# A Mamba-2 convolution tile: four products on ScalarE, three additions on GpSimd

## The reference, cut to what matters

```python
def causal_dwconv(xpad, w, bias):
    K = w.shape[0]
    T = xpad.shape[1] - K + 1
    y = bias
    for j in range(K):
        y = y + xpad[:, j:j + T] * w[j]
    return y

def ssd_mixer(z, xbc, dt_raw, conv_buf, h0, conv_w, conv_b, dt_bias, A_log, D_skip, norm_w):
    ...
    xpad = jnp.concatenate([conv_buf.astype(xbc.dtype), xbc], axis=1)
    xbc_c = jax.nn.silu(causal_dwconv(xpad, conv_w, conv_b))
    ...
    xs, Bm, Cm = jnp.split(xbc_c, [C_INNER, C_INNER + C_GROUPS * C_STATE], axis=-1)
    ...
    y, h_new = ssd_scan(xs, dt, A, Bm, Cm, h0.astype(F32))
```

## Time and profile before

| | |
|---|---|
| median of three runs | 3177.0 us |
| the profiled execution, its own time | 3178.87 us |
| its span | 3177.1 us |
| mean granted TensorE clock | 0.971 of full |
| `local_stage`, first `convolve_x` to last matmul | 1083 to 1372 us |
| PE, DVE, ACT, POOL busy over the span | 94%, 51%, 27%, 24% |

### The profile page before, as it was taken

One profiled execution on the slowest core, in us unless ns is written; L12 is line 12 of the kernel. 1 busy time (PEld: TensorE's weight loads), 2 busy tenths in 40 slices (PEclk: granted clock), 3 DMA queues, 4 the chain that ended last, 5 costly groups with the idle time before them and its releaser, 6 DMA issues. The chain is left out here.

```text
span 3177.1 us, 45320 instructions
## 1 busy us (share of the span) xinstructions
PE 2986.0 (94%) x16451; PEld 2559.2 (81%) x16451; DVE 1618.7 (51%) x3026; ACT 867.5 (27%) x1660; POOL 749.8 (24%) x512
## 2 busy tenths in 40 slices
PE   8999999789899799978979999999998999999998
PEld 5888889666666599866769999999996788888886
DVE  5113211266678488856645555545556444444445
ACT  4223222223332255533342211112213111111112
POOL 4002100134444145522201222111221121122210
PEclk9999999889999899989989999999999999999999
DMA  4455335367674244338652111121113311111101
GB/s 147 165 210 178 111 128 176 91 187 210 196 211 140 86 120 116 88 93 266 199 205 102 40 40 40 40 79 40 40 53 137 115 53 40 40 40 59 60 13 54
DMA packets 237378, 350.26 MB, mean 110 GB/s; under 512 B 75334, under 2 KB 172135, under 8 KB 231256
## 3 DMA queue, kind: packets, MB, share of 16 engines
q1 hardware_dynamic: 236289, 325.80, 33.1%
q0 software_dynamic: 944, 22.61, 1.9%
HBM read 283.53 MB, written 93.97 MB: 119 GB/s over the span
## 5 line engine op out<-in xcount | busy, mean ns | idle before, releaser
L2558 POOL TENSOR_TENSOR cm_dn_lo<-cm_dn_raw,cm_dn_hi 128x1024 fp32r<-128x1024 f32 x44 | 107.8, 2470 | 972.1 <-ACT cm_dn_hi L2607 972.1
L3288 PE MATMUL pj_acc<-pj_w_hi,pj_h_hi 128*128 128x480 f32 (+3 forms) x896 | 335.5, 374 | 0.9 <-DVE pj_h_lo L3163 0.9
L3289 PE MATMUL pj_acc<-pj_w_lo,pj_h_hi 128*128 128x480 f32 (+3 forms) x896 | 333.9, 373 | 0.0
L3290 PE MATMUL pj_acc<-pj_w_hi,pj_h_lo 128*128 128x480 f32 (+3 forms) x896 | 333.7, 372 | 0.0
L2851 PE MATMUL cm_u_ps<-cm_h_hi,cm_up_hi 128*128 128x344 f32 (+1 forms) x880 | 309.5, 352 | 12.6 <-DVE cm_a_lo L2724 12.6
L2851 PE MATMUL cm_g_ps<-cm_h_hi,cm_up_hi 128*128 128x344 f32 (+1 forms) x880 | 310.3, 353 | 11.3 <-DVE cm_h_lo L2663 10.9
L2853 PE MATMUL cm_u_ps<-cm_h_hi,cm_up_lo 128*128 128x344 f32 (+1 forms) x880 | 308.7, 351 | 0.0
L2853 PE MATMUL cm_g_ps<-cm_h_hi,cm_up_lo 128*128 128x344 f32 (+1 forms) x880 | 308.7, 351 | 0.0
L2852 PE MATMUL cm_u_ps<-cm_h_lo,cm_up_hi 128*128 128x344 f32 (+1 forms) x880 | 307.9, 350 | 0.0
L2852 PE MATMUL cm_g_ps<-cm_h_lo,cm_up_hi 128*128 128x344 f32 (+1 forms) x880 | 307.9, 350 | 0.0
L3169 DVE TENSOR_TENSOR pj_w_lo<-pj_w_raw,pj_w_hi 128x480 fp32r<-128x480 f32 (+3 forms) x112 | 75.7, 697 | 377.8 <-ACT pj_w_hi L3125 377.7
(11 more groups left out here) (447 smaller groups left out, 6484.8 us busy)
## 6 DMA issues: line engine op xcount, KB each, us to landing
fp_kv<-in_fox_kv SPq DMA_DIRECT2D x256, 256.0 KB, 3.0
area<-in_w_up SPq DMA_DIRECT2D x44, 1024.0 KB, 7.1
cm_dn_raw<-in_w_down SPq DMA_DIRECT2D x44, 512.0 KB
out_s_win<-in_cache POOLq DMA_DIRECT2D x8, 2047.0 KB, 9.3
proj_a<-pj_row SPq DMA_DIRECT2D x48, 240.0 KB
sp_raw<-proj_b SPq DMA_DIRECT2D x16, 640.0 KB, 4.0
pj_w_raw<-in_w_a SPq DMA_DIRECT2D x10, 960.0 KB, 7.0
dp_raw<-proj_a SPq DMA_DIRECT2D x48, 192.0 KB, 3.8
```

What stands on the lines that cost most here:

```text
L2558: pool.tensor_tensor(dn_lo[:, s], dn_raw[:, s], dn_hi[:, s].bitcast(F32), ALU.subtract).then_inc(dn_ready, 1)
L3288: pe.matmul(out, h_hi[:, k, place(t)], w_hi[:, j % 2, k, 0:wide], start=(k == 0), stop=False)
L3289: pe.matmul(out, h_hi[:, k, place(t)], w_lo[:, j % 2, k, 0:wide], start=False, stop=False)
L3290: last = pe.matmul(out, h_lo[:, k, place(t)], w_hi[:, j % 2, k, 0:wide], start=False, stop=(k == KT - 1))
```

## The change

ScalarE gets a function `multiply_taps`, called in phase 1 behind `sp_z_tanh`. It makes the four products of the third x tile, each into its own part of `sp_x_part`, which grows from one to four tiles; the first product takes the bias with it (Identity with scale and bias, both per-partition), the others are Copy with a per-partition scale. GpSimd's `convolve_x` waits for all four (a new semaphore `taps_done`) and makes three additions. The waits for `xT`, the halo and the earlier readers move to ScalarE with the products; for chunk 0 ScalarE waits for `diag_ready` as well, which comes after the taps were halved. `mask` and everything else stays where it was in its queue.

```diff
-        x_part = sb("sp_x_part", [P, P])
+        x_part = sb("sp_x_part", [P, C_CONV, P])
...
+        taps_done = sem("sp_taps_done")
...
             def convolve_x(c):
-                pool.wait_ge(in_ready, 2 * c + 1)
-                pool.wait_ge(halo_ready, c + 1)
-                if c >= 1:
-                    pool.wait_ge(s_ready, 2 * c - 1)
                 k = XT - 1
-
-                def tap(j):
-                    return taps[:, k, j:j + 1].to_broadcast([P, P])
-
-                gps.link(pool, pool.tensor_tensor(x_conv[:, k], xT[:, c % 2, k, 0:P], tap(0), ALU.mult))
-                gps.link(pool, pool.tensor_tensor(x_conv[:, k], x_conv[:, k], tap(C_CONV), ALU.add))
-                for j in range(1, C_CONV):
-                    gps.link(pool, pool.tensor_tensor(x_part[:], xT[:, c % 2, k, j:j + P], tap(j), ALU.mult))
-                    last = pool.tensor_tensor(x_conv[:, k], x_conv[:, k], x_part[:], ALU.add)
-                    if j < C_CONV - 1:
-                        gps.link(pool, last)
-                last.then_inc(x_conv_ready, 1)
+                pool.wait_ge(taps_done, c + 1)
+                gps.link(pool, pool.tensor_tensor(x_conv[:, k], x_part[:, 0], x_part[:, 1], ALU.add))
+                gps.link(pool, pool.tensor_tensor(x_conv[:, k], x_conv[:, k], x_part[:, 2], ALU.add))
+                pool.tensor_tensor(x_conv[:, k], x_conv[:, k], x_part[:, 3], ALU.add).then_inc(x_conv_ready, 1)
...
+            def multiply_taps(c):
+                k = XT - 1
+                act.wait_ge(halo_ready, c + 1)
+                act.wait_ge(in_ready, 2 * c + 1)
+                if c >= 1:
+                    act.wait_ge(s_ready, 2 * c - 1)
+                else:
+                    act.wait_ge(diag_ready, 1)
+                act.activation(x_part[:, 0], xT[:, c % 2, k, 0:P], ACT.Identity, scale=taps[:, k, 0:1],
+                               bias=taps[:, k, C_CONV:C_CONV + 1])
+                for j in range(1, C_CONV):
+                    last = act.activation(x_part[:, j], xT[:, c % 2, k, j:j + P], ACT.Copy, scale=taps[:, k, j:j + 1])
+                last.then_inc(taps_done, 1)
...
                     act.activation(z_tanh[:], raw[:, now % 2, CZ:CX], ACT.Tanh, scale=0.5).then_inc(z_tanh_ready, 1)
+                    multiply_taps(now)
```

## The result

The changed kernel took 3181.48 us (median of 20 runs, 3174.61 to 3193.5), the kernel before in the same comparison 3177.85: a ratio of 1.0018, with a 95% interval of 1.0009 to 1.0026, or 2.9 to 8.3 us more. 3183.0 was forecast.

What follows compares the result with a forecast made beforehand. In the changed stage TensorE (98% busy) and VectorE (87%) were taken as near their limit. Chunk delays at L1332 sum to +6.2, rounded to +6.0 us, taking the median from 3177.0 to 3183.0; range 3172 to 3190.

Steps and rivals of the forecast that it cites:

- The gauge and the slack: TensorE's wait at turn_x for VectorE's sp_y (L1332): 2.9 us growing to some 9; handover 0.15, slack 0.40 or none.
- the first kind: Chunks 1 to 5 and 9, where VectorE's L1332 comes early for turn_x: 0.40 us of slack each, 2.3 us lost together.
- ScalarE's four products: On ScalarE ahead of copy_out: four 128x128 instructions take 1.36 us, at no cost because ScalarE then idles 2.59 us.
- The added wait: GpSimd's first addition waits for taps_done: starts at 1181.07 against 1180.94 in chunk 5, 1319.87 against 1319.53 in chunk 13.
- The mask and who goes first: GpSimd's mask starts about 2.6 us sooner and goes before VectorE's last L1262 or sp_z: +1.2 us chunk 5, +1.3 chunk 13.
- The relief behind it: VectorE instructions after sp_z, no longer beside the mask, run faster: -0.41 us chunk 5, about -0.65 or -0.85 in later ones.
- The sum: Delay at L1332 over the stage's chunks: 2.3, 0.8, 2.0, 1.35, -0.2 and 0, total +6.2 us, rounded to +6.0.
- Chunk 0: 0: At the stage's start the taps wait for diag, but VectorE and turn_x have over 1.5 us of slack: 0 us.
- (a): Rival, faster: VectorE passes before the mask, TensorE's waits before L1426 vanish, -4.6 us to 3172.4; chance 0.15.
- (b): Rival, no change: the mask wins in some chunks and loses in others, cancelling within 2 us, 3177; chance 0.14.
- (c): Rival, much slower: ScalarE's taps_done comes late, each 0.4 us delaying additions and mask in all 16 chunks, 3189; chance 0.07.
- (d): Rival: ScalarE's Identity wants another table, two loads of 1.28 us a chunk, 3177 + 41 = 3218; chance 0.02.

Runs made afterwards that it cites:

- spare_taps: Kernel before plus ScalarE's four products, written to a tile nothing reads; GpSimd unchanged. Ratio 0.9993, median 3175.9 us.
- changed_again: The changed kernel, unaltered, timed once more beside other runs on one chip. Ratio 1.0005, median 3181.6 us.
- diag_first: Kernel before, with GpSimd's convolve_x of chunk 0 waiting for diag_ready. Ratio 0.9992, median 3176.4 us.
- mask_after_z: Changed kernel, with the mask of chunk c+1 also waiting until VectorE's sp_z of chunk c is done. Ratio 0.9977, median 3170.5 us.
- mask_early_late_start: Changed kernel with the mask moved to phase 0 and the mask of chunk 1 waiting for diag_ready. Ratio 0.9966, median 3167.9 us.
- mask_early: Changed kernel with GpSimd's mask moved from phase 2 to phase 0, behind sp_xdd. Ratio 0.9971, median 3170.9 us.
- adds_alone: Kernel before with GpSimd's eight instructions replaced by three additions, no ScalarE products, computing other numbers. Medians 3178.4 and, repeated, 3177.7 us.
- more_before_mask: Changed kernel plus one unread GpSimd product of 128x384 between the additions and the mask. Ratio 1.003, median 3187.2 us.

## Why the prediction was right

**The gauge and the slack.** Right. The 0.15 handover is there in all chunks of the changed kernel, and the first kind lost its 0.40 of slack before it lost time: the wait before `turn_x` in chunks 1 to 5 and 9 is 0.39 or 0.40 each, 2.4 in sum for the 2.3 forecast.

**ScalarE's four products.** Right: 0.48 and three of 0.39, 1.37 us where 1.36 was forecast. The row of the exponential had given that number. By the formula of the Trainium skill ("ScalarE: Activation LUTs", What ACT_TABLE_LOAD costs) it was 1.36 as well, and this trace agrees with its 0.479 us for the first and 0.386 for each of the others. They cost nothing: the chunks and the stage of spare_taps are as long as those of the kernel before.

**The added wait.** Right: the first addition starts 1.85 us behind the start of `sp_z_tanh` in chunk 5 (1172.73 against 1170.88) and in chunk 13; 1.85 was forecast for both.

**The mask and who goes first.** Right, and this was the guess with the most weight. In chunks 1 to 11 the last tap, in 12 to 14 `sp_z` waited out the mask, in every one of them. `sp_z` ended 1.20 us later in chunk 5 and 1.30 later in chunk 13, counted from `sp_z_tanh`; 1.2 and 1.3 were forecast.

**The relief behind it.** Right. From the end of `sp_z` to that of L1336 it is 4.71 us in chunk 5 instead of 5.10 (-0.39, forecast -0.41), 4.08 in chunk 13 instead of 4.93 (-0.85, as forecast).

**The sum.** By kinds, from the waits before `turn_x`: +2.4 (2.3), chunk 8 +0.8 (0.8), chunks 6, 7, 10 and 11 together +2.0 (2.0), 12 to 14 +1.3 (1.35), chunk 15 -0.2 (-0.2). The distance over all chunks grew by 6.5 for 6.2.

**What was missed** are two terms at the ends, -1.8 and +1.9 us. That they cancel, so that the whole stage too came out 6.6 us longer, is luck. Chunk 0 and the start were put at nothing; the faster build of the diagonal matrices gave 1.8 us back. The step of the prediction that failed is "Chunk 0: 0": I looked for slack behind the products and not at what their going away relieves. And the tail, from the last `sp_xd` to L1518, took 12.6 us instead of 10.7. The granted clock is 0.72 on the mean in 4 us of it, that is a part of the stretch at the lower level (1.2 GHz); before it was 1.00 there. Ahead of the fall TensorE had been idle for 0.69 and 0.89 us, with matmuls between; the kernel before has the same two idle times at this place and kept its level. The clock (last figure but two) in these 4 us and in the whole tail, of the changed kernel and of the kernel before:

```profile
1360.00:1364.00 4.00, 2.85 (x16) 2.71 (x16) 1.17 (x8) 2.13 (x9) 1.76 (x2) 0.72 0.29 83
1357.83:1370.38 12.55, 8.95 (x55) 8.47 (x55) 6.80 (x27) 5.45 (x23) 3.57 (x4) 0.81 0.12 33
```

```profile
1363.00:1367.00 4.00, 2.70 (x24) 2.56 (x24) 2.01 (x14) 2.13 (x9) 2.52 (x3) 1.00 0.34 99
1361.32:1371.98 10.66, 6.90 (x55) 6.42 (x55) 6.72 (x27) 5.45 (x23) 3.56 (x4) 1.00 0.15 40
```

The same 55 matmuls take 8.95 us instead of 6.90, while ScalarE's work is the same and VectorE's nearly so. Over all 13 traces the tail's length goes with its clock: 10.7 us at 1.00, 11.1 at 0.94 and 0.95, 11.7 at 0.85, 12.1 at 0.86, 12.6 at 0.81, 13.1 at 0.74. The long tail came again in changed_again (12.6), but also in diag_first (12.1), mask_after_z and mask_early_late_start (13.1 each), and not in mask_early, adds_alone or more_before_mask. What makes the clock fall in one kernel and not in another stays open. So does the size of the loss in the total: the stage is 6.4 to 6.6 us longer in both traces of the changed kernel, the two comparisons have their centres at 5.7 and 1.6, nothing behind the stage is shorter, and what lies ahead of it differs by up to 13 us from trace to trace.

**The rivals.** (a) is refuted in chunks 1 to 14, all that have a mask behind them, and so is (b) as a mechanism: the mask won in every one of them. Its "no change" in the total is what the second comparison alone can't exclude. (c) and (d) didn't come, with `taps_done` in time and no table load in the stage (the first after 577 us is at 1380.6).

## What to carry to other kernels

Where VectorE is close to its limit, count GpSimd's instructions not by their time but by what VectorE does beside them: a long one in a bad place cost VectorE most of its length here (1.2 to 1.3 us of 1.5), and even an instruction of 128x2 waited for it. Taking work away from GpSimd moves what stands behind it in its queue, and that may land worse. Look for the stretch in which VectorE reads PSUM or waits, and put GpSimd's longest instruction there: that one move gained 5 us in the kernel before, and with it the changed kernel is 9 us under the kernel before, where the edit alone had lost some 2 to 6.

## What the runs showed of the hardware

In chunks 1 to 15, VectorE's instructions with two SBUF inputs and GpSimd's took turns, one instruction each, and where VectorE waited it ended 0.14 to 0.15 us (128 columns) or 0.42 (384) behind GpSimd's end. At two places of the kernel before the two start within 0.01 us of each other, and each had one outcome in all of chunks 1 to 15: `sp_z`, with an immediate scalar, went before L1052; L1262, with a per-partition scalar, went behind L1050. Whether the kind of scalar is the reason isn't shown. The Trainium skill ("SBUF — State Buffer", Who interferes with whom) has the exclusive lock, and the traces here agree with it. By its rule of whoever issues first, taken by the start times of the profile, the L1262 of 1181.46 should have gone before the L1050 of 1181.47, and it didn't.

VectorE's instructions from SBUF to SBUF with one input and a scalar were held as well: those of the diagonal matrices (0.49 to 0.55 us beside a small GpSimd instruction, 1.56 beside the mask, 0.28 alone) and `dp_neg` of 128x2 (0.84 beside the mask, 0.17 alone).
